# Expert rows by indirect DMA with lists of row numbers, in place of slot-matrix products on the matmul engine

## The reference, cut to what matters

```python
def moe_swiglu(h, router, w_gate, w_up, w_down):
    t = h.reshape(b * s, d)                               # 256 tokens x 1024
    top_logits, top_idx = lax.top_k(t @ router, TOP_K)    # 2 of 8 experts per token
    top_w = jax.nn.softmax(top_logits, axis=-1)
    combine = jnp.einsum('tk,tke->te', top_w, jax.nn.one_hot(top_idx, N_EXPERTS))
    out = jnp.zeros_like(t)
    for e in range(N_EXPERTS):
        out = out + combine[:, e:e + 1] * swiglu(t, w_gate[e], w_up[e], w_down[e])
    return out                                            # the caller adds x
```

## Time and profile before

| what | value |
|---|---|
| time, median of 3 runs | 1716.63 us (1714.97 to 1717.34) |
| span of the profiled execution | 1715.5 us, 1.1 us under the median |
| mean granted PE clock | 0.983 |
| start of the first job's products on PE | 688.8 us |
| start of the same in the second job | 815.9 us |
| from the first to the second | 127.1 us |
| last result's copy on ACT to the end of the span | 10.3 us |

### The profile page before, as it was taken

One profiled execution on the slowest core, in us unless ns is written; L12 is line 12 of the kernel. 1 busy time (PEld: TensorE's weight loads), 2 busy tenths in 40 slices (PEclk: granted clock), 3 DMA queues, 4 the chain that ended last, 5 costly groups with the idle time before them and its releaser, 6 DMA issues.

```text
span 1715.5 us, 25622 instructions
## 1 busy us (share of the span) xinstructions
PE 1643.5 (96%) x9426; PEld 1309.6 (76%) x9426; DVE 1299.3 (76%) x1509; ACT 1092.9 (64%) x1295; POOL 23.1 (1%) x22
## 2 busy tenths in 40 slices
PE   6978999999899999999999999999999999999998
PEld 6857999998898988677677677677677677676675
DVE  4465555454588774898898898898998998998996
ACT  3655444444455463777777777777777777777774
POOL 0000000000002100000000000000000000000000
PEclk9999999999899999999999999999999999999999
DMA  7422444554243246799899899999999999999980
GB/s 268 167 79 99 152 168 177 197 185 160 98 165 132 99 160 233 284 367 375 299 368 363 307 371 349 321 368 339 335 367 332 336 373 331 336 373 333 334 312 26
DMA packets 185851, 447.76 MB, mean 261 GB/s; under 512 B 3736, under 2 KB 4106, under 8 KB 185786
## 3 DMA queue, kind: packets, MB, share of 16 engines
q1 hardware_dynamic: 184656, 444.61, 71.8%
q0 software_dynamic: 448, 1.26, 0.3%
q10 hardware_dynamic: 682, 0.99, 0.2%
HBM read 445.78 MB, written 1.06 MB: 260 GB/s over the span
## 4 chain that ended last, share of the span: by engine, by line
PE 91%; DVE 4%; ACT 2%; issue 1%; DMA 0%; POOL 0%; DVEq 0%; ACTq 0%
PE bank L571 89%; PE bank L904 1%; DVE split_mem L1672 0%; DMA mem<-x 0%; ACT split_mem L1248 0%; DVE mem L1379 0%; DVE mem L1308 0%; POOL mem L562 0%; ACT mem L1030 0%; DVE mem L1463 0%; ACT split_mem L990 0%; DVE split_mem L1340 0%; DVE mem L1495 0%; PE bank L594 0%; DVE mem L1507 0%
## 5 line engine op out<-in xcount | busy, mean ns | idle before, releaser
L571 PE MATMUL bank<-split_mem 128*128 128x256 f32 (+1 forms) x8064 | 1463.2, 342 | 24.3 <-DVE split_mem L1324 9.9
L571 PEld LDWEIGHTS bank<-split_mem 128*128 128x128 f32 (+1 forms) x8064 | 1145.5, 178 | 312.8 <-issue 27.8
L1695 DVE TENSOR_TENSOR split_mem<-mem,split_mem 128x1024 fp32r<-128x1024 f32 x672 | 817.5, 1223 | 110.7 <-ACT split_mem L1248 97.4
L1248 ACT CAST split_mem<-mem 128x1024 fp32r<-128x1024 f32 x672 | 706.9, 1052 | 246.8 <-PE bank L571 246.0
L1340 DVE TENSOR_TENSOR split_mem<-mem,split_mem 128x1024 fp32r<-128x1024 f32 x172 | 210.6, 1229 | 197.2 <-ACT split_mem L990 197.1
L990 ACT CAST split_mem<-mem 128x1024 fp32r<-128x1024 f32 x172 | 179.8, 1048 | 222.5 <-PE bank L571 222.3
L571 PE MATMUL bank<-mem 128*128 128x96 f32 (+7 forms) x704 | 110.8, 335 | 10.4 <-DVE mem L1308 5.6
L571 PEld LDWEIGHTS bank<-mem 128*128 128x128 f32 (+3 forms) x704 | 82.1, 189 | 30.0 <-issue 27.2
L571 PE MATMUL bank<-mem,cst 128*128 128x256 f32 (+2 forms) x134 | 40.7, 450 | 9.5 <-ACT mem L969 4.6
L1702 DVE TENSOR_TENSOR mem<-mem,bank 96x512 f32<-96x512 f32 x56 | 37.9, 677 | 0.0
L571 PEld LDWEIGHTS bank<-mem,cst 128*128 128x128 f32 x134 | 25.2, 199 | 16.6 <-issue 14.1
(11 more groups left out here) (152 smaller groups left out, 406.1 us busy)
## 6 DMA issues: line engine op xcount, KB each, us to landing
mem<-moe_w_gate SPq DMA_DIRECT2D x56, 2048.0 KB, 7.8
mem<-moe_w_up SPq DMA_DIRECT2D x56, 2048.0 KB, 7.9
mem<-moe_w_down SPq DMA_DIRECT2D x56, 2048.0 KB, 7.9
mem<-ssd_w_in SPq DMA_DIRECT2D x10, 2048.0 KB, 7.9
mem<-ffn_w_gate SPq DMA_DIRECT2D x7, 2048.0 KB, 7.7
mem<-ffn_w_up SPq DMA_DIRECT2D x7, 2048.0 KB, 7.8
mem<-ffn_w_down SPq DMA_DIRECT2D x7, 2048.0 KB, 7.9
mem<-attn_w_in SPq DMA_DIRECT2D x6, 2048.0 KB, 8.6
```

Source lines behind the costliest of these rows:

```text
L571: return nc.tensor.matmul(o, lhsT, rhs, start=start, stop=stop, skip_group_check=shared)
L1248: nc.scalar.copy(wsplit[:, EXPERT_BUFFER[n % EXPERT_SPLITS], 0, :].rearrange("p (k n) -> p k n", n=w.shape[2]), quarter(w, q)).then_inc(w_ ...
L1695: tt_(lo, quarter(w, q), hi.bitcast(F32), ALU.subtract).then_inc(w_lo, 1)
```

## The change

The residual rows `xnat` and the normed rows `hnat` are written to DRAM by POOL before the first job: `xnat` straight to the output, `hnat` to a new tensor `h_rows`. For each job a list of 96 row numbers and 96 weights is made (`slot_list` on PE, two products of the slot matrix with a table; DVE copies it out in `next_list` and makes it current in `take_list`). `fetch_rows` on POOL reads the 96 rows of the next job by an indirect DMA into `hrow`, and PE only transposes them (`turn_rows`). ACT's `copy_result` multiplies by the slot's weight. `add_rows` on POOL adds the 96 result rows to the output by an indirect DMA that accumulates. Scatter, `PT`, `add_result` and the last write of the output are gone. Every slot gets a token of its own: those that the expert did not choose stand behind the chosen ones, with weight 0.

```diff
+            def add_rows(job):
+                pool.wait_ge(y_ready_e, 2 * (job + 2))
+                if job:
+                    pool.wait_ge(summed, 16 * (job + 1))
+                pool.indirect_dma_start(out[0], bass.IndirectOffsetOnAxis(this_token, 0), ynat[0:SLOTS, :], None,
+                                        compute_op=ALU.add).then_inc(summed, 16)
+            def fetch_rows(job):
+                pool.wait_ge(list_ready, job + 1)
+                if job > 1:
+                    pool.wait_ge(in_hrow, 16 * (job - 1))
+                pool.indirect_dma_start(hrow[0:SLOTS, :], None, h_rows, bass.IndirectOffsetOnAxis(next_token, 0))\
+                    .then_inc(in_hrow, 16)
...
-            gather(0)
-            pe.wait_ge(no_result, 1)
+            gather_first()
+            def slot_list():
+                for tt in range(TT):
+                    last = mm(bank[7][0:SLOTS, 0:JOBS + 1], Pm[:, tt, :], cj[:, tt, :], tt == 0, tt == 1)
+                return last
+            pe.wait_ge(table_ready, 1)
+            B.claim(pe, "list0")
+            B.finish(slot_list(), "list0")
+            def turn_rows(job):
+                pe.wait_ge(in_hrow, job * 16 + 16)
+                for half in range(2):
+                    b = 1 + 2 * half
+                    for q in range(4):
+                        d = 4 * half + q
+                        last = nc.tensor.transpose(bank[b][:, q * SLOTS:(q + 1) * SLOTS],
+                                                   hrow[0:SLOTS, d * P:(d + 1) * P], cst[0:SLOTS, 0:SLOTS])
+                    last.then_inc(full[b], 1)
...
-                    else:
-                        scatter(job)
                     projected("up", c, 2 + c % 2)
-                    if c == 1:
-                        job_claim(pe, "PT", job)
-                        for tt in range(TT):
-                            last = nc.tensor.transpose(bank[7][0:SLOTS, tt * P:(tt + 1) * P], Pm[:, tt, :], C("ident"))
-                        last.then_inc(full[7], 1)
+                    if c == 2:
+                        job_claim(pe, "list", job)
+                        pe.wait_ge(place_ready, job + 2)
+                        slot_list().then_inc(full[7], 1)
...
-                gather(job + 1)
+                turn_rows(job)
                 down_chunk(NC_F - 1)
...
+                act.wait_ge(this_ready, job + 1)
                 for half in range(2):
-                    nc.scalar.copy(ynat[0:SLOTS, half * 512:(half + 1) * 512], bank[4 + half][0:SLOTS, :])\
-                        .then_inc(y_ready_e, 1)
+                    fn(ynat[0:SLOTS, half * 512:(half + 1) * 512], bank[4 + half][0:SLOTS, :], ACT.Identity,
+                       scale=this_weight).then_inc(y_ready_e, 1)
...
+            B.ready(dve, "list0")
+            V_.tensor_copy(next_token, bank[7][0:SLOTS, 0:1])
+            B.release(V_.tensor_copy(next_weight, bank[7][0:SLOTS, 1:2]), "list0")
+            B.released(dve, "list0")
+            V_.tensor_copy(small[:, 31:32], small[:, 24:25]).then_inc(list_ready, 1)
...
+            def take_list(job):
+                dve.wait_ge(summed, job * 16 + 16)
+                dve.wait_ge(list_ready, job + 1)
+                V_.tensor_copy(this_token, next_token)
+                V_.tensor_copy(this_weight, next_weight).then_inc(this_ready, 1)
+            def next_list(job):
+                job_ready(dve, "list", job)
+                dve.wait_ge(this_ready, job + 2)
+                V_.tensor_copy(next_token, bank[7][0:SLOTS, 0:1])
+                V_.tensor_copy(next_weight, bank[7][0:SLOTS, bass.ds(job + 2, 1)]).then_inc(free[7], 1)
+                job_released(dve, "list", job)
+                V_.tensor_copy(small[:, 31:32], small[:, 24:25]).then_inc(list_ready, 1)
...
-                    if tile == ("up", 0):
-                        add_result(job)
...
+                    if tile == ("up", 1):
+                        take_list(job)
+                        places(job + 1)
+                    if tile == ("up", 3):
+                        next_list(job)
```

More of the change, by code:

```diff
@@ L59 @@
                   ("mean_g", 128), ("upto", 128), ("before", 128), ("ones", 128), ("slot_no", SLOTS),
-                  ("rank_of", E), ("eps", 1), ("one", 1), ("odd_even", 128), ("pair_of", 16)):
+                  ("rank_of", E), ("eps", 1), ("one", 1), ("odd_even", 128), ("pair_of", 16), ("token", 2)):
     CONSTS[_name] = (_at, _at + _n)
@@ L92, in constants @@
     put("pair_of", i[:, None] // 2 == np.arange(16)[None, :])
+    put("token", i[:, None] + P * np.arange(2)[None, :])
     dist = 255 - np.arange(NDIST)
@@ L217, in hybrid_trunk @@
         relb = sb("relb", [BUCKETS + 1, HEADS])
-        flag = sb("flag", [P, 2], I32)
+        flag = sb("flag", [P, 4], I32)
         tables = sb("tables", [P, 768])
@@ L369, in hybrid_trunk @@
             B.plan(("hnat", i), 4 + i)
-        B.plan("logits", 0), B.plan("rank", 1)
+        B.plan("logits", 0), B.plan("rank", 1), B.plan("list0", 7)
         dense_uses = list(B.count)
-        SCATTER_BANK = [7, 6, 4, 5]
         J = Banks(full, free, None)
-        for i in range(4):
-            J.plan(("sc", i), SCATTER_BANK[i])
         for c in range(NC_F):
@@ L382, in hybrid_trunk @@
         J.plan(("gather", 0), 1), J.plan(("gather", 1), 3)
-        J.plan("PT", 7)
+        J.plan("list", 7)
         USES = list(J.count)
@@ L447, in hybrid_trunk @@
         place_ready = sem("place_ready")
+        list_ready, this_ready = sem("list_ready"), sem("this_ready")
+        in_h_rows, in_hrow = sem("in_h_rows"), sem("in_hrow")
+        summed = sem("summed")
         hg_hi = sem("hg_hi")
@@ L565, in _, with jobs @@
                                             ALU.mult).then_inc(ce_ready, 1)
+            for i in range(4):
+                B.released(pool, ("hnat", i))
+            pool.dma_start(h_rows.rearrange("(a p) n -> p a n", p=P), hnat[:, :, :]).then_inc(in_h_rows, 16)
+            for i in range(4):
+                B.released(pool, ("xnat", i))
+            pool.dma_start(out[0].rearrange("(a p) n -> p a n", p=P), xnat[:, :, :]).then_inc(summed, 16)
+            pool.wait_ge(in_h_rows, 16)
+            pool.wait_ge(summed, 16)
+            def add_rows(job):
[10 more added lines that the diff above has]
+                    .then_inc(in_hrow, 16)
+            def jobs(first, end):
+                for job in range(first, end):
+                    if job:
+                        add_rows(job - 1)
+                    fetch_rows(job + 1)
+            jobs(0, E)
+            pool.wait_ge(flag_ready, 1)
+            more = pool.value_load(flag[0:1, 0:1], min_val=0, max_val=1)
+            with pool.If(more > 0):
+                jobs(E, JOBS)
+                add_rows(JOBS - 1)
+                pool.wait_ge(summed, 16 * (JOBS + 1))
+                pool.wait_ge(in_hrow, 16 * JOBS)
+            with pool.Else():
+                add_rows(E - 1)
+                pool.wait_ge(summed, 16 * (E + 1))
+                pool.wait_ge(in_hrow, 16 * E)
         @block.tensor
@@ L839, in _, with gather_first @@
             B.finish(mm(bank[1][:, 2 * E:3 * E], C("ones"), sel[:, E:2 * E], False, True), "rank")
-            def gather(job):
-                pe.wait_ge(place_ready, job + 1)
+            def gather_first():
+                pe.wait_ge(place_ready, 1)
                 for half in range(2):
@@ L892, in down_chunk @@
                     if c == 0:
-                        for i in (2, 3):
-                            job_released(pe, ("sc", i), job)
+                        pe.wait_ge(y_ready_e, job * 2 + 2)
                     job_released(pe, ("hidT", c), job)
@@ L935, in _ @@
                     job_body(job)
-            scatter(more * (JOBS - E) + E)
         @block.scalar
@@ L1265, in job_body @@
                         copy_result(job)
-                    if tile == ("gate", 2):
-                        job_ready(act, "PT", job)
-                        nc.scalar.copy(PT[0:SLOTS, :, :], bank[7][0:SLOTS, 0:T]).then_inc(free[7], 1)
                 hidden_hi(NC_F - 1)
@@ L1627, in _ @@
             dve.wait_ge(sel_ready, 1)
[L1628 to L1633, removed]
+            ahead = bank[1][:, 0:2 * E].rearrange("p (t e) -> p t e", e=E)
+            token = C("token").unsqueeze(2).broadcast_to([P, TT, E])
+            behind = per_expert(tw[:, 11, :])
+            link(tt_(behind, bank[1][:, 2 * E:3 * E].unsqueeze(1).broadcast_to([P, TT, E]), token, ALU.add))
+            stt(out=tmp, in0=ahead, scalar=2.0, in1=behind, op0=ALU.mult, op1=ALU.subtract)
+            link(stt(out=behind, in0=ahead, scalar=-1.0, in1=behind, op0=ALU.mult, op1=ALU.add))
+            link(tt_(tmp, tmp, sel, ALU.mult))
+            place = rj[:, :, 0:E]
+            link(tt_(place, behind, tmp, ALU.add))
             link(V_.tensor_reduce(tw[:, 0, E:E + 1], bank[1][:, 2 * E:3 * E], AX_X, ALU.max))
@@ L1651, in _ @@
```

(18 more changed lines are left out.)

15 lines of the change are left out of this document (6 added, 9 removed).

## The result

The changed kernel takes 1691.65 us (median of four runs, 1688.14 to 1695.27). The kernel before took 1716.99 beside it. The ratio is 0.9851, with a 95% interval of 0.9835 to 0.9867, so it is 1.5% faster. The forecast was 1689.

A forecast was written before the change was run, and what follows sets the result against it. PE was taken to bound the expert stage, with DVE close behind. Eight jobs gain 28.8 us, the end gains 2.5, the start loses 3.6: 27.7 us off 1716.6 gives 1689 us, range 1682 to 1696, or 1673 to 1712 with two rivals.

The forecast's parts named there:

- Scatter: Between gate 0 and up 0 of each job: removing PE's scatter saves 3.1 us a job, the splits keeping up.
- the lists: On PE, two float32 products replace two slot-matrix transposes: 0.1 to 0.2 us lost a job.
- Gather: Before down 6: eight transposes replace it, 0.7 us saved a job; about 1.9 us become PE's wait on DVE.
- Per job: In the expert stage: 3.1 + 0.7 - 0.2 us gained in each of eight jobs, giving jobs of 123.5 us.
- Ahead of the first job: Before the first products: DVE waits for the first list, 3.6 us lost once.
- The half-speed stretch: At the first job's start: PE's clock at half for 6 us would cost 3 us more; kept for the range.
- The end: After the last copy's start: copy and one accumulating DMA, taken as 7.8 us against 10.3, gain 2.5 us.
- ACT's copy with a weight: On ACT: the same two instructions of 0.53 us as before.
- the DMA engines as the bound: Rival: indirect DMAs take 17 us of engine time a job, jobs of 130.8 us, about 1718 us; chance 0.03.
- POOL does not hold DVE up: Rival denied here: each indirect DMA holds DVE for 2 us, giving 1700 us, up to 1712; chance 0.17.
- The late add: Rival: take_list on DVE waits for the accumulating DMA; 1731 us at a latency of 26 us; chance 0.15.
- the wait behind the gather might not show: Rival before down 6: DVE reaches hidden_lo(6) earlier, saving 1.9 us a job more, 1674 us; chance 0.05.

The follow-up runs named there:

- e3: Changed kernel with PE's gather by the slot matrix kept in every job and nothing fetched; lists and accumulating DMAs stay: 1694.33 us, ratio 0.9868.
- e1: Changed kernel with hidden_hi(6) on ACT and hidden_lo(6) on DVE put ahead of the last quarter's split of down 6: 1676.54 us, ratio 0.9775.
- e7: Changed kernel with the last hidden chunk ahead of the last quarter's split, and the first list made between the first gather's halves: 1676.72 us, ratio 0.9765.
- e4: Changed kernel with three plain 0.39 MB DMAs, one after the other, ahead of each accumulating DMA: 1773.1 us in a single run.
- e6: Changed kernel with POOL also copying the 1 MB of h_rows with each fetch: once 1693.93 us, ratio 0.9869; three times 1692.4 us in a single run.
- e5: Changed kernel with one plain 0.39 MB DMA ahead of each accumulating DMA: 1695.28 us, ratio 0.9885.

## Why the prediction was right

**Scatter.** Forecast 3.1 us a job less 0.1 to 0.2 for the lists, measured 3.3 net (e3). The step was right, and 0.3 to 0.4 us too small. The splits kept up without the pause, as read.

**Gather.** Forecast 0.7 us a job and a new wait of about 1.9; measured 0.7 and 1.95. This was the step on which the sum turned. By instruction times alone it would have been 2.6 us a job and 1674 in all. What was missed is the price of the new idleness in clock: four cuts of 1.2 to 1.6 us in this profile, 5.5 together.

**Per job** that makes 123.1 us where 123.5 was forecast, and 123.8 on average over the last seven with the cuts (816.41 to 1682.80 between the adds' issues). From the second job's first product to the last result's copy, 889.3 us became 866.7: 22.7 gained where 7 x 3.6 = 25.2 was forecast. Two misses of opposite sign meet here, jobs that are 0.4 us shorter than forecast and the cuts of the clock.

**Ahead of the first job.** Forecast 3.6 us lost before the first products. Measured from the first `places` to them: 11.4 us against 7.35, so 4.1 lost. 1.0 of this is the gather, which took 6.43 us in this profile and 5.41 before; with a gather of 5.41, as in e1 and e3, 3.1 are lost. The half-speed stretch that I kept for the range did come, and in the whole segment to the second job 2.3 us are lost where the sum had 0.

**The end.** 1690.6 - 1681.3 = 9.3 us against 10.3: 0.9 gained, 2.5 forecast. The add took about 7.8 us from its issue to the end of the span; ACT's copy and the hand-over to POOL were 1.5. My term was mis-sized: 10.3 - 7.8 = 2.5 takes the 7.8 for copy and add together, which left 6.7 us for the add.

**Together**, 22.7 + 0.9 - 2.3 = 21.3 us in this profile, where the sum had 27.7. The other 3.6 of its 24.9 arose ahead of the first `places` (677.8 against 681.4) and can't be put down to the change: with the same code up to there, `places` stood at 679.7 in e1, 681.8 in e7 and 682.0 in e3. The medians of the runs are 25.3 us apart; how much of that is such chance I can't tell from one profile each. So the mechanism of the prediction held, but that the time came within 3 us of 1689 is in part luck.

**Slips that cost nothing.** ACT's copy with a weight is not the same as before, 1.25 us for its two instructions against 1.06. And 1718 us for the DMA engines as the bound does not follow from its terms: 8 x (130.8 - 123.5) - 26 = 32 us, so 1721.

**The rivals.** POOL does not hold DVE up. Sixteen indirect DMAs take 1.1 to 1.7 us each on POOL, all but the last of them beside DVE's splits, and none of the 672 splits took longer than 1.228 us (1.228 before too). So the Trainium skill's rule (SBUF — State Buffer, section Who interferes with whom) on GpSimd instructions that read SBUF did not show with a DMA that reads a list of 96 numbers. The advice in the summary of the same page of the Trainium skill, which the prediction put beside that rule, is given for the other direction: there it is the DMA's descriptor generation that starves while DVE is in a 2x or 4x mode. So it did not bear on this rival. The late add is a real deadline, and the add had some 8 us to spare (done 9.8 us behind ACT's copy, against 18.2 in e4). The DMA engines had room (e6). The doubt that the wait behind the gather might not show was unfounded.

## What to carry to other kernels

Before an instruction is taken off the engine that bounds the kernel, look for what other engines finish while it runs. Here 1.9 of the 2.6 us that the removal saved on PE were cover for a chain of DVE work, and with two lines moved on ACT and DVE the removal came to 2.1 us a job (e1 against e3). An idle stretch that is put on PE can cost more than its own length: behind one of 1.95 us the granted clock was at half in four of eight jobs, 1.2 to 1.6 us each. And an indirect accumulating DMA of 0.39 MB beside a stream of weights landed in 6.9 to 9.7 us over these runs. That is free where its deadline, read off the timeline first, is later.

## What was not expected of the hardware

Behind waits of 1.95 us once in 123 us the granted clock was at half in four of eight jobs, and behind waits of 0.58 us (e1, e7) in none. With the gather kept (e3) it was 1.00 in all the later jobs too. The number is not fixed by the wait: the same 1.95 us had four such jobs in the profile of one copy (e6), one each in those of three copies and of e5, and seven in e4. So "four" is one execution's number. What decides which jobs stays open.

An indirect DMA kept POOL for only 1.1 to 1.7 us in the changed kernel, and the accumulating one (9.5 us to landing) was hardly slower than the plain fetch (8.8 us). Behind a plain DMA of the same rows (e5) it landed in 6.9 us; why stays open.
